# Sixteen pairs of feed-forward tiles as 2x2 blocks with seven products in place of eight

## The reference

```python
h2 = rmsnorm(x, norm_pre_ffn) * (1 + sc2) + sh2
fg, fu = jnp.split(h2 @ w_ffn_in, 2, axis=-1)      # 1024 -> 2 x 2816
ff = (jax.nn.silu(fg) * fu) @ w_ffn_out            # 2816 -> 1024
x = x + g2 * rmsnorm(ff, norm_post_ffn)
```

## Time and profile before

| | us |
|---|---|
| median of 3 runs | 1426.11 (1425.17 to 1426.21) |
| profiled execution, device time | 1426.0 |
| its span, first to last instruction | 1424.2 |
| TensorE busy | 1373.5 (96%) |
| VectorE busy | 718.2 (50%) |
| ScalarE busy | 484.0 (34%) |
| mean granted TensorE clock | 0.985 of full |

### The profile page before, as it was taken

How to read it: one execution, slowest core, us unless ns; L and a number is a source line. 1 busy time by engine, 2 the same in 40 slices (tenths; PEclk the granted TensorE clock), 3 DMA queues, 4 the chain that set the end, 5 groups by cost and what they waited for, 6 DMA issues and landing times.

```text
span 1424.2 us, 24013 instructions
## 1 busy us (share of the span) xinstructions
PE 1373.5 (96%) x10324; PEld 1278.4 (90%) x10324; DVE 718.2 (50%) x998; ACT 484.0 (34%) x683; POOL 177.0 (12%) x284
## 2 busy tenths in 40 slices
PE   6899999999999999999999999998899999999995
PEld 3899999888986998898799879997899999999995
DVE  4458888522243663375248526966733333332225
ACT  4476778221322412231233124354422222222221
POOL 1122231000124123213222230000000000000000
PEclk8899999999999999999999999999999999999998
DMA  9422122682525245424443442361022222223221
GB/s 360 149 75 89 61 76 85 247 307 83 190 82 191 97 134 175 143 75 147 150 156 103 135 152 96 94 228 43 15 75 89 89 90 89 88 71 92 86 82 63
DMA packets 49930, 172.70 MB, mean 121 GB/s; under 512 B 5537, under 2 KB 7713, under 8 KB 49569
## 3 DMA queue, kind: packets, MB, share of 16 engines
q1 hardware_dynamic: 39456, 135.51, 28.2%
q0 software_dynamic: 9216, 33.56, 7.1%
q10 hardware_dynamic: 1152, 2.10, 0.4%
HBM read 149.82 MB, written 21.32 MB: 120 GB/s over the span
## 4 chain that ended last, share of the span: by engine, by line
PE 85%; DVE 9%; ACT 3%; issue 2%; DMA 1%; POOL 0%; SPq 0%; DVEq 0%; ACTq 0%; POOLq 0%
PE ps L770 69%; PE ps L779 3%; PE ps L1015 2%; PE ps L1026 2%; PE ps L818 1%; PE ps L998 1%; PE ps L1058 1%; PE ps L1044 1%; PE ps L901 1%; DMA raw<-in_w_out 1%; DVE w_lo L1536 1%; ACT w_hi L1199 1%; PE ps L955 1%; PE ps L968 0%; DVE hs L1653 0%
## 5 line engine op out<-in xcount | busy, mean ns | idle before, releaser
L770 PE MATMUL ps<-h_hi,w_hi 128*128 128x272 f32 x2096 | 442.3, 292 | 7.5 <-DVE h_lo L1555 5.2
L770 PE MATMUL ps<-h_hi,w_lo 128*128 128x272 f32 x2096 | 435.1, 289 | 0.0
L770 PE MATMUL ps<-h_lo,w_hi 128*128 128x272 f32 x2096 | 433.7, 288 | 0.0
L1536 DVE TENSOR_TENSOR w_lo<-raw,w_hi 128x1024 fp32r<-128x1024 f32 (+2 forms) x190 | 226.5, 1195 | 312.1 <-ACT w_hi L1199 309.7
L770 PEld LDWEIGHTS ps<-h_hi,w_hi 128*128 128x128 f32 x2096 | 332.3, 189 | 21.0 <-issue 12.4
L770 PEld LDWEIGHTS ps<-h_lo,w_hi 128*128 128x128 f32 x2096 | 330.9, 189 | 0.0
L770 PEld LDWEIGHTS ps<-h_hi,w_lo 128*128 128x128 f32 x2096 | 328.8, 190 | 0.0
L1199 ACT ACTIVATE w_hi<-raw 128x1024 fp32r<-128x1024 f32 (+2 forms) x190 | 195.6, 1030 | 337.7 <-PE ps L770 245.6
L1813 DVE SCALAR_TENSOR_TENSOR state<-state,ps 128x512 f32<-128x512 f32 x64 | 41.1, 684 | 108.1 <-PE ps L1058 107.9
L770 PE MATMUL ps<-a_hi,w_hi 128*128 128x272 f32 x308 | 63.8, 288 | 2.5 <-DVE a_lo L1545 2.5
L770 PE MATMUL ps<-a_hi,w_lo 128*128 128x272 f32 x308 | 63.8, 288 | 0.0
(11 more groups left out here) (244 smaller groups left out, 1843.6 us busy)
## 6 DMA issues: line engine op xcount, KB each, us to landing
raw<-in_w_head SPq DMA_DIRECT2D x48, 512.0 KB, 3.9
raw<-in_w_fin SPq DMA_DIRECT2D x38, 512.0 KB, 3.4
state<-in_state POOLq DMA_DIRECT2D x32, 512.0 KB, 4.5
out_rs<-state POOLq DMA_DIRECT2D x32, 512.0 KB, 4.0
raw<-in_w_rnn SPq DMA_DIRECT2D x24, 512.0 KB, 3.5
ada_more<-in_w_ada SPq DMA_DIRECT2D x23, 512.0 KB, 7.8
ada_raw<-in_w_ada SPq DMA_DIRECT2D x16, 512.0 KB, 14.9
raw<-in_w_bret SPq DMA_DIRECT2D x16, 512.0 KB, 3.4
```

What stands on the lines that cost most here:

```text
L770: mm = nc.tensor.matmul(dst[:, half, :], a, b[:, half * HALF:(half + 1) * HALF], start=first and j == 0, stop=last and j == 2)
L1536: V.tensor_tensor(lo[:, 0:cols], raw_slab(i)[0][:, 0:cols], hi[:, 0:cols].bitcast(F32), ALU.subtract).then_inc(lo_ready, 1)
```

## The change

Pairs of tiles n = 6 to 21 (FIRST = 6, PAIRS = 16) are taken as a 2x2 block product. A11 and A12 are the k 0 to 3 and k 4 to 7 parts of gate slab n, A21 and A22 those of up slab n; the input is likewise cut into four blocks, by k and by half of the tokens. In place of eight block products (each 4 k, one half) there are seven, with weight sums S1 = A21 + A22, S3 = A11 + A21 (made by transfers that add to what was loaded), S2 = S1 + A11 and S4 = S2 + A12 (made by VectorE), and with four sums XA to XD of the input, made once. Products are partly accumulated in the banks; ScalarE copies four of the partial sums out, VectorE combines them into gate and up tile (the up tile with the opposite sign, which the gating takes back).

What moves with it: `mo` and `x_res` become the memory of the input sums' parts `x_lo` and `x_hi`, so x1 is stored to the output y and loaded again behind the last product; `keep` writes the biased input back into `mo`; the parts of the slab A22 lie in the place of a part of `h_hi`/`h_lo` that is no longer read; the parts of the output tiles' slabs wait for the last pair's products; the output tile ("fo", 0) waits for the hidden layer k by k.

```diff
+FIRST = 6
+PAIRS = NF - FIRST
+PRODUCTS = 7
+BLOCK = KD // 2 * P
...
@@ SyncE @@
+            load_to(pl.slab[("fu", EARLY, "w", 0)])
+            sp.wait_ge(x1_ready, 2 * KD)
+            sp.dma_start(out["y"], xr_[:]).then_inc(x1_stored, 16)
+            load_to(last_plain)
+            def load_blocks(p):
+                n, u = FIRST + p, p % 2
+                if p < 2:
+                    of_slot = [i for i in pl.kinds["raw"] if i <= last_plain and pl.place[i][1] % RAW == u]
+                    sp.wait_ge(lo_ready, of_slot[-1] + 1)
+                else:
+                    sp.wait_ge(blocks_ready, 4 * (p - 2) + 1)
+                sp.dma_start(raw[:, u, :], w["w_fin"][n, 0]).then_inc(a11_in[u], 16)
+                if p < 2:
+                    sp.wait_ge(h_ready, 3 * KD)
+                else:
+                    sp.wait_ge(blocks_ready, 4 * (p - 2) + 2)
+                sp.dma_start(s13_raw[:, u, 0, :], w["w_fin"][n, 1][:, 0:BLOCK]).then_inc(s1_in[u], 16)
+                sp.dma_start(s13_raw[:, u, 1, :], w["w_fin"][n, 1][:, 0:BLOCK]).then_inc(s3_in[u], 16)
+                if p:
+                    sp.wait_ge(blocks_ready, 4 * (p - 1) + 4)
+                sp.dma_start(a22_raw, w["w_fin"][n, 1][:, BLOCK:2 * BLOCK]).then_inc(a22_in, 16)
+            for p in range(PAIRS):
+                load_blocks(p)
+            for i in range(RAW):
+                of_set = [p for p in range(PAIRS) if p % 2 == pl.place[last_plain + 1 + i][1] % RAW]
+                sp.wait_ge(blocks_ready, 4 * of_set[-1] + 1)
+                load_to(last_plain + 1 + i)
+            sp.wait_ge(product_done, products_until(PAIRS, 0))
+            sp.wait_ge(x1_stored, 16)
+            sp.dma_start(xr_[:], out["y"]).then_inc(xres_in, 16)
...
@@ TensorE @@
-            for n in range(EARLY, NF):
+            for n in range(EARLY, FIRST):
                 project(("fg", n), [KD], h_hi, h_lo)
                 project(("fu", n), [KD], h_hi, h_lo)
-            pe.wait_ge(a_ready, 2 * EARLY + NF - EARLY)
+            def product(bank, block, name, add=False):
+                for k in range(KD // 2):
+                    whi, wlo = (block_columns(w, h, block, k) for w, h in ((w_hi, h_hi), (w_lo, h_lo)))
+                    xh, xl = x_block(h_hi, x_hi, name)[:, k, :], x_block(h_lo, x_lo, name)[:, k, :]
+                    for j, (a, b) in enumerate(((whi, xh), (whi, xl), (wlo, xh))):
+                        mm = nc.tensor.matmul(ps[:, bank, 0:HALF], a, b, start=not add and k == 0 and j == 0,
+                                              stop=k == KD // 2 - 1 and j == 2, skip_group_check=True)
+                mm.then_inc(product_done, 1)
+            for p in range(PAIRS):
+                q, s, t = product_banks(p)
...
+                if p >= 2:
+                    pe.wait_ge(banks_read, p - 1)
+                pe.wait_ge(blocks_ready, 4 * p + 1)
+                product(q, "A11", "B11")
+                if p == 0:
+                    wait_took(pe, ("fu", FIRST - 1))
+                    pe.wait_ge(x_ready, 1)
+                pe.wait_ge(blocks_ready, 4 * p + 2)
+                product(t, "S1", "XC")
+                if p == 0:
+                    pe.wait_ge(x_ready, 4)
+                pe.wait_ge(blocks_ready, 4 * p + 3)
+                pe.wait_ge(part_copied, 4 * p + 1)
+                product(q, "S2", "XA", add=True)
+                product(s, "A12", "B21")
+                pe.wait_ge(part_copied, 4 * p + 3)
+                product(q, "S3", "XB", add=True)
+                product(t, "S4", "B22", add=True)
+                pe.wait_ge(blocks_ready, 4 * p + 4)
+                pe.wait_ge(part_copied, 4 * p + 4)
+                product(q, "A22", "XD", add=True)
...
@@ ScalarE @@
+            def keep(half):
+                at = prompt_of(half)
+                for k in range(KD):
+                    act.wait_ge(h_ready, KD * (1 + half) + k + 1)
+                    do(A(mo[:, k, at], mo[:, k, at], ACT.Identity, bias=mod[:, 3 * KD + k, 0:1]), h_kept, wait=False)
...
             silu_half(0, 0)
+            keep(0)
             for k in range(KD):
                 square_of_sum(1, k)
...
             for n in range(EARLY):
                 silu_half(n, 1)
+            keep(1)
+            def hi_of_blocks(p, slab):
+                if p == PAIRS:
+                    split_to(last_plain + 1 + slab)
+                    return
+                u, loaded = p % 2, 16 * (p // 2 + 1)
+                if slab == 0:
+                    act.wait_ge(a11_in[u], loaded)
+                elif slab == 1:
+                    act.wait_ge(s1_added[u], loaded)
+                    act.wait_ge(s3_added[u], loaded)
+                elif slab == 2:
+                    act.wait_ge(sums_ready, p + 1)
+                else:
+                    act.wait_ge(a22_in, 16 * (p + 1))
+                if p:
+                    act.wait_ge(product_done, products_until(p - 1, 4 + slab))
+                else:
+                    act.wait_ge(multiplied, pl.tile_end[(("fu", FIRST - 2), ("fg", FIRST - 1), ("fu", FIRST - 1),
+                                                         ("fu", FIRST - 1))[slab]])
+                do(A(blocks_to(w_hi, h_hi, slab), blocks_from(p, slab), ACT.Copy), blocks_hi, wait=False)
+            def copy_part(p, i, product):
+                act.wait_ge(product_done, products_until(p, product))
+                if p:
+                    act.wait_ge(row_made, 3 * (p - 1) + (1, 2, 3, 2)[i])
+                q, _, t = product_banks(p)
+                do(A(copied(i), ps[:, t if i == 1 else q, 0:HALF], ACT.Copy), part_copied, wait=False)
...
+            for p in range(PAIRS):
+                if p < 1:
+                    hi_of_blocks(p, 2)
+                if p:
+                    gate_pair(p - 1)
+                hi_of_blocks(p, 3)
+                copy_part(p, 0, 1)
+                if p:
+                    hi_of_gated(p - 1)
+                copy_part(p, 1, 2)
+                copy_part(p, 2, 3)
+                hi_of_blocks(p + 1, 0)
+                copy_part(p, 3, 5)
+                hi_of_blocks(p + 1, 1)
+                hi_of_blocks(p + 1, 2)
...
@@ VectorE @@
+            def sums_of_weights(p):
+                u, loaded = p % 2, 16 * (p // 2 + 1)
+                a11, a12 = raw[:, u, 0:BLOCK], raw[:, u, BLOCK:2 * BLOCK]
+                s2, s4 = s24_raw[:, 0, :], s24_raw[:, 1, :]
+                dve.wait_ge(a11_in[u], loaded)
+                dve.wait_ge(s1_added[u], loaded)
+                do(V.tensor_tensor(s2, s13_raw[:, u, 0, :], a11, ALU.add))
+                do(V.tensor_tensor(s4, s2, a12, ALU.add), sums_ready)
...
+            for n in range(EARLY, FIRST):
+                plain_ahead(("fg", n))
+                if n == EARLY:
+                    sums_of_input()
+                plain_ahead(("fu", n))
+                if n < FIRST - 1:
+                    plain_gated(n)
+            sums_of_weights(0)
+            lo_of_blocks(0, 0)
+            lo_of_blocks(0, 1)
+            for p in range(PAIRS):
+                lo_of_blocks(p, 2)
+                if p:
+                    gated_pair(p - 1)
+                else:
+                    plain_gated(FIRST - 1)
+                lo_of_blocks(p, 3)
+                if p:
+                    lo_of_gated(p - 1)
+                if p + 1 < PAIRS:
+                    sums_of_weights(p + 1)
+                first_row(p, 0)
+                lo_of_blocks(p + 1, 0)
+                second_row(p)
+                lo_of_blocks(p + 1, 1)
+                first_row(p, 1)
...
@@ GpSimd @@
+            for p in range(PAIRS):
+                n, u = FIRST + p, p % 2
+                pool.wait_ge(s1_in[u], 16 * (p // 2 + 1))
+                pool.dma_start(s13_raw[:, u, 0, :], w["w_fin"][n, 1][:, BLOCK:2 * BLOCK], accum_op=ALU.add)\
+                    .then_inc(s1_added[u], 16)
+                pool.wait_ge(s3_in[u], 16 * (p // 2 + 1))
+                pool.dma_start(s13_raw[:, u, 1, :], w["w_fin"][n, 0][:, 0:BLOCK], accum_op=ALU.add)\
+                    .then_inc(s3_added[u], 16)
```

More of the change, by code:

```diff
@@ L571, in took_half, with place_of, blocks_to, blocks_from @@
             return took(pl.half_tile[key][0])
+        last_plain = pl.slab[("fu", FIRST - 1, "w", 0)]
+        def place_of(slab):
+            return (pl.ringed.index(last_plain) + 1 + slab) % RING
+        def blocks_to(w, h, slab):
+            if slab == 3:
+                return h[:, 0:2, HALF:HALF + BLOCK // 2]
+            return w[:, place_of(slab), :].rearrange("p (b c) -> p b c", b=2)
+        def blocks_from(p, slab):
+            if slab == 3:
+                return a22_raw.rearrange("p (b c) -> p b c", b=2)
+            if slab == 2:
+                return s24_raw
+            if slab == 1:
+                return s13_raw[:, p % 2, :, :]
+            return raw[:, p % 2, :].rearrange("p (b c) -> p b c", b=2)
+        def block_columns(w, h, name, k):
+            if name == "A22":
```

(40 more changed lines are left out.)

108 lines of the change are left out of this document (95 added, 13 removed).

## The result

The changed kernel takes 1405.72 us, the median of four runs (1405.04 to 1407.11), against 1426.16 before: a ratio of 0.985 (95% interval 0.982 to 0.988), 20.4 us less. 1401.9 was forecast, with a likeliest range of 1400.5 to 1405 and a whole one of 1400 to 1411. The direction and the mechanism were right; 3.8 us of the gain are missing, and the time lies 0.7 us above the likeliest range, inside the whole one.

A forecast was written before the change was run, and what follows sets the result against it. The prediction took TensorE's number of matmuls as the bound. Terms of -24.1, -2.5, +1.7 and +0.7 sum to -24.2 us, taking 1426.1 to 1401.9 us; likeliest range 1400.5 to 1405, whole range 1400 to 1411.

The forecast's parts named there:

- 192 matmuls: Sixteen pairs at 84 matmuls in place of 96, each 0.1253 us: -24.1 us.
- wait for the whole hidden layer: Behind the last pair: TensorE's 2.47 us wait goes, as the first output tile waits k by k: -2.5 us.
- pair 0's bank: Pair 0's second product waits until up tile 5's bank is read: +1.7 us, bounds 1.5 and 2.2.
- the slab behind the reload: First output tile's slab 2, loaded behind the reload of x1, comes late: +0.7 us, bounds 0 and 2.
- (a): In each pair a copy, high or low part reaches TensorE 0.3 to 1 us late: 1407 to 1418; chance 0.13.
- (b): Accumulating transfer sets the two-pair loop, landing in 9 to 11 us: 1409 to 1423 us; chance 0.09.
- (d): Pitch rises to 0.143 with one half per weight load, so fewer matmuls don't pay: about 1424; chance 0.02.
- The steady pair: Pairs of 10.53 us, VectorE 8.8 and ScalarE 6.6 busy, smallest margin 1.05 us at the copies; priced at nothing.
- The accumulating transfers: GpSimd's weight-sum additions land in 4.5 us, bounds 3.1 and 10.1; no cost up to about 8 us.
- (c): Accumulating transfer lands in 12 us or more, making the kernel slower: 1433 us at 12.5; chance 0.05.
- Ahead of the first pair: Write-backs of the biased input, input sums and the x1 store before pair 0 stay hidden: no cost.

The follow-up runs named there:

- eight products again: Changed kernel with the fourth product issued twice into the same bank, so a pair has 96 matmuls: 1430.57 us.
- k by k alone: Kernel before the change, with only the first output tile waiting for the hidden layer k by k: 1426.51 us against 1429.4 (0.998).
- slab first: Changed kernel with SyncE loading two more output-tile slabs ahead of the reload of x1: 1401.93 us (ratio 0.983).
- run with copies: Changed kernel with GpSimd's transfers copying in place of adding, sums S1 and S3 left out of the computation: 1406.98 us.

## Why the prediction was right, and by how much it missed

| step | forecast | measured | by |
|---|---|---|---|
| 192 matmuls | -24.1 | -24.1 | eight products again |
| wait for the whole hidden layer | -2.5 | -3.0 | k by k alone |
| pair 0's bank | +1.7 | +1.8 | wait; -2.2 when taken away |
| the slab behind the reload | +0.7 | +5.9 | slab first |
| sum | -24.2 | -19.4 | stage: -18.7; 0.7 is open |

**Where luck helped.** The whole range reached to 1411 to take in rivals (a) and (b), and neither came; what used its room is a term at the reload that was given 2 us at most and cost 5.9. And 2.3 us of the profiled difference were no gain of the change. The likeliest range was also narrower than its own terms, which give 1401.0 to 1406.6 and not 1400.5 to 1405.

**The count.** The pitch of 0.1253 us held for products (168.47 us for 1344 matmuls, 0.1254), and with it the largest term. Rival (d) is out.

**The steady pair** went as laid out. The first copy was forecast to end at 1.95 us and the sums at 5.5; counted from the first matmul of a pair (1141.09), they ended at 2.1 and 5.5. No wait of TensorE stands in fifteen pairs. Rival (a), late hand-overs, did not happen. VectorE's room was 1.5 us a pair, and 2.2 us more work overran it by what was forecast for such a case.

**The step that failed** is the one behind the last pair, a mis-sized term with a wait that I did not name. The transfer was nearly right: 0.4 + 9.5 us behind the last product forecast, 0.4 + 9.9 measured (issues at 1246.55 and 1246.93), which is most of the way from the 0.7 us forecast to the 1.3 that the transfer alone makes. But I added only the slab's own high and low part. On ScalarE the slab's high part is queued *ahead* of the last pair's SiLU; ScalarE stood 12.1 us before it with finished products behind it, and VectorE does that pair's gating before the slab's low part. So 0.55 + 0.45 + 0.45 + 0.67 + 0.74 us, with hand-overs 3.1, came between high and low part: ScalarE's order alone is worth 3.0 us of wait. The second omission is the clock. The wait of 2.5 us before the change left it at 1.00, so did the 3.1 of one experiment; the 4.3 us were followed by 0.58. That is the 1.6 us between 4.3 and 5.9.

**The accumulating transfers.** The landing was taken as 4.5 and measured 4.1 and 5.4, and rivals (b) and (c) did not come about, for which TensorE's waits are the witness. The *distance* to them was badly wrong, though. I had put the threshold at a landing of 7 to 8 us. SyncE's plain loads landed in 5.4 us, not in 3.4. Of that 0.8 comes with the additions, since the same loads take 4.6 in the run with copies; the rest, doubled traffic or the place in a row of four loads, is not parted by any run. That place alone puts S1's load 0.85 us behind A22's (1145.25 and 1144.40), which my sum left out. In the pair at 1155 S1 was there 0.3 us before the sums began, not 2.6; in the other pairs from the third on it was 0.3 to 1.7 us early, and in one VectorE did wait for it, though TensorE did not:

```profile
1188.57 0.69 DVE L2228 TENSOR_TENSOR a_mem<-s_raw,raw 128x512 f32<-128x512 f32 x1 [1.31 <-DMA s_raw<-in_w_fin]
```

And the loop has a second branch, S3 to ScalarE's high part, which I left out. Put off by 1.35 us, the additions cost 9.7 us; by 3.2, the whole gain and more. The rule of the Trainium skill that I had weighed (page "SBUF — State Buffer", section "SBUF: two separate sides": descriptors of GpSimd's transfers wait while VectorE is in a two-port mode) is not seen at work here: with VectorE busy for 10.74 of 11.29 us, nearly all of it two-input operations, the landings were 4.3 and 5.5 us at the median against 4.1 and 5.4. No run here shows the copy that the page gives as its example, so the rule itself is not put to the test.

**Ahead of the first pair** nothing was exposed, as forecast: tiles 3 to 5 are one piece of 288 matmuls in 36.10 us.

## What to carry to other kernels

Where TensorE's matmuls stand end to end, fewer matmuls pay at their pitch, and laying out one period on every engine tells whether it holds. At the seams count everything that is queued behind the engine that waits, not just the late item's own way: a late transfer of 1.3 us became 4.3 and then 5.9. A loop that TensorE never waits for can still be within half a microsecond of setting the time; putting one link off by a known time is a cheap way to find out.

## What was not expected of the hardware

- An accumulating transfer of 256 KB lands 0.8 to 2.1 us later than a plain one from the same queue (4.1 and 5.4 against 3.3 us), and takes GpSimd 0.86 and 1.12 us to issue in place of 0.54.
- Plain loads of 256 KB on SyncE's queue, issued in a row of four, landed in 5.4 us at a DMA share of 0.69 and in 4.6 at 0.55; before, 512 KB issued alone took 3.4 us at 0.27.
- At the same bytes, two of a pair's six transfers as additions and not as copies raised the DMA share from 0.55 to 0.69.
- TensorE's granted clock stayed at 1.00 after gaps of 1.3, 2.5 and 3.1 us ahead of or in the first output tile, and was 0.58 to 0.62 over the 4 us that followed gaps of 4.3 and 4.1 us. The length of the gap alone does not decide: in the changed kernel a gap of 2.8 us near the end, from 1386.79 on, was followed by 0.50, with two matmuls in the next 4 us.
